# Prompt attention of a hybrid decoder layer: value products by twos, four slots for turned weights, and a new order of rows, turns and values

## The reference

```python
def block(i):                                   # 128 queries at a time
    s = (einsum('bqhd,bkhd->bhqk', qn, k_nope)  # 16 heads, 64 + 32 wide
         + einsum('bqhr,bkr->bhqk', qp, k_pe)) * ATTN_SCALE
    s = where(key_pos[None, :] <= q_pos[:, None], s, finfo.min)
    p = softmax(s, axis=-1)
    return einsum('bhqk,bkhd->bqhd', p, v)      # values 64 wide
```

## Time and profile before

| what | value |
|---|---|
| runs (median, lowest, highest) | 2851.91, 2851.1, 2855.4 us |
| profiled execution | 2861.62 us, span 2859.8 us |
| mean granted TensorE clock | 0.987 of 2.4 GHz |
| PE, PEld busy | 2781.5 us (97%), 2532.8 us (89%) |
| DVE, ACT, POOL busy | 1500.8 us (52%), 752.1 us (26%), 1056.5 us (37%) |
| prompt attention: L1373, L1388, L1398 in the chain that ended last | 3%, 2%, 3% of the span |

### The profile page before, as it was taken

The page is one execution under the profiler, slowest core; times in us unless marked ns, Lnnn a source line. Parts: engine busy times, 40 slices in busy tenths (PEclk is TensorE's granted clock), DMA queues, the critical chain, the costliest instruction groups (busy, mean ns, idle before and its releaser), DMA issues.

```text
span 2859.8 us, 45005 instructions
## 1 busy us (share of the span) xinstructions
PE 2781.5 (97%) x18648; PEld 2532.8 (89%) x18648; DVE 1500.8 (52%) x2075; ACT 752.1 (26%) x1182; POOL 1056.5 (37%) x611
## 2 busy tenths in 40 slices
PE   7999999999999999999999899999999999999998
PEld 7999999998999896666666599999999999999998
DVE  3665888674766564555444447876642222222226
ACT  2221211363545543555423322101210000000000
POOL 2553333333333333555311123446433333333331
PEclk9999999999999999999999999999999999999999
DMA  5274223564756657444343524354211111111111
GB/s 145 92 273 168 83 83 115 173 182 145 182 154 176 162 161 177 109 104 125 144 181 151 187 93 143 110 182 123 68 45 45 45 45 45 45 48 48 45 52 61
DMA packets 332053, 337.13 MB, mean 118 GB/s; under 512 B 43168, under 2 KB 284069, under 8 KB 329638
## 3 DMA queue, kind: packets, MB, share of 16 engines
q1 hardware_dynamic: 266984, 211.97, 26.6%
q10 hardware_dynamic: 61302, 84.71, 8.3%
q0 software_dynamic: 3584, 37.75, 3.4%
HBM read 245.35 MB, written 89.02 MB: 117 GB/s over the span
## 4 chain that ended last, share of the span: by engine, by line
PE 56%; DVE 5%; ACT 2%; issue 2%; DMA 2%; ACTq 0%; POOL 0%; DVEq 0%; SPq 0%
PE ps L1042 35%; PE ps L1373 3%; PE ps L1236 3%; PE ps L1398 3%; PE ps L1388 2%; PE ps L1530 2%; PE ps L1487 2%; PE ps L1506 1%; PE ps L1654 1%; DMA kpb<-in_cache_kpe,pgx 1%; ACT prb L2067 1%; DVE alo L2761 0%; DMA gt<-d_z 0%; DMA d_y<-s_y 0%; DVE ytok L2987 0%
## 5 line engine op out<-in xcount | busy, mean ns | idle before, releaser
L841 POOL TENSOR_TENSOR whi<-raw,cst 128x1024 fp32r<-128x1024 f32 x160 | 319.6, 1998 | 1084.5 <-PE ps L1042 888.8
L843 POOL TENSOR_TENSOR wlo<-raw,whi 128x1024 fp32r<-128x1024 f32 x160 | 432.8, 2705 | 12.5
L1042 PE MATMUL ps<-ahi,whi 128*128 128x352 f32 x1728 | 376.4, 326 | 1.9 <-DVE alo L2761 1.9
L1042 PE MATMUL ps<-alo,whi 128*128 128x352 f32 x1728 | 376.5, 326 | 0.0
L1042 PE MATMUL ps<-ahi,wlo 128*128 128x352 f32 x1728 | 371.6, 324 | 0.0
L1042 PEld LDWEIGHTS ps<-ahi,whi 128*128 128x128 f32 x1728 | 295.3, 190 | 2.5 <-DVE alo L2761 2.5
L1042 PEld LDWEIGHTS ps<-ahi,wlo 128*128 128x128 f32 x1728 | 297.1, 190 | 0.0
L1042 PEld LDWEIGHTS ps<-alo,whi 128*128 128x128 f32 x1728 | 296.1, 189 | 0.0
L1236 PE MATMUL ps<-xhi,whi 128*128 128x352 f32 x768 | 255.2, 332 | 2.8 <-ACT zo L1904 2.8
L1236 PE MATMUL ps<-xlo,whi 128*128 128x352 f32 x768 | 249.5, 325 | 0.0
L1236 PE MATMUL ps<-xhi,wlo 128*128 128x352 f32 x768 | 247.7, 323 | 0.0
(11 more groups left out here) (378 smaller groups left out, 5052.5 us busy)
## 6 DMA issues: line engine op xcount, KB each, us to landing
raw<-in_w_in SPq DMA_DIRECT2D x61, 512.0 KB, 5.5
s_a<-d_acum SPq DMA_DIRECT2D x32, 512.0 KB, 7.2
d_xbc<-so ACTq DMA_DIRECT2D x24, 528.0 KB, 2.7
gt<-d_g SPq DMA_DIRECT2D x24, 528.0 KB, 3.6
raw<-in_w_ffn_gate SPq DMA_DIRECT2D x22, 512.0 KB, 3.8
raw<-in_w_ffn_up SPq DMA_DIRECT2D x22, 512.0 KB, 3.8
raw<-in_w_ffn_down SPq DMA_DIRECT2D x22, 512.0 KB, 3.7
d_z<-zo ACTq DMA_DIRECT2D x16, 528.0 KB, 5.0
```

Of the source, the lines that this page charges most:

```text
L841: pool.tensor_tensor(whi[s][:, :], raw[:, u], ones[:, 0:1].broadcast_to([P, UNIT]), ALU.mult).then_inc(sem("unit_hi"), k["unit_hi"].adds(1))
L843: pool.tensor_tensor(wlo[s][:, :], raw[:, u], whi[s][:, :].bitcast(F32), ALU.subtract).then_inc(sem("unit_split"), k["unit_split"].adds(1))
L1042: last = pe.matmul(ps[0:m, 3 * b + c, 0:width], w(j), x[:, j, at:at + width], start=i == 0, stop=i == n - 1)
```

## The change

- `weigh_two` takes two key blocks' values together, a block and the one below it. Before it, PE waits for the copies: `turned_since` says how many turns have been issued since the second of the two; 0 waits for all copies, 1 for all but the last.
- `ptb` has four slots for each head in place of two. The two new ones lie where the split weights of other stages and `wrow` lie. `slot_of` picks one: `(4G + 3 - kb_) % 4`.
- The order of rows, turns and values is written anew on PE, and the order of maxima, reciprocals, exponentials and copies on DVE and ACT with it. After a turn there now often stand one or two rows, or another turn, where a weigh stood. `head_out` of half 1 stands before the exponential of row (1,1), and that of half 0 between those of (1,6) and (1,7).
- SP waits for the last values (`o_ready` at 16) before it loads `wrow`.

```diff
@@ -448,11 +448,15 @@
-    ptb = [[ar(f"ptb{slot}{h}", [P, 512]) for h in range(2)] for slot in range(2)]
+    idle_weights = Arena(base + RAW * UNIT * 4)
+    ptb = [[at(f"ptb{slot}{h}", [P, 512]) for h in range(2)] for slot, at in enumerate((ar, ar, idle_weights, idle_weights))]
...
+    def slot_of(G, kb_):
+        return (4 * G + 3 - kb_) % 4
@@ -759,6 +763,7 @@
         next_weights(4)
+        sp.wait_ge(sem("o_ready"), HEADS)
@@ -1395,34 +1400,64 @@
+        def weigh_two(pp, G, kb_, turned_since):
+
+            for h in range(2):
+                pe.wait_ge(sem(f"pt_read{h}"), k[f"pt_read{h}"].value(turned_since))
+            weigh(pp, G, kb_)
+            weigh(pp, G, kb_ - 1)
+
         def later_rows(pp, final=False):
-            for i in range(8):
-                scores(pp, 1, i)
-                if i % 2 == 0:
-                    turn_probs(0, 3 - i // 2)
-                    if i:
-                        weigh(pp, 0, 4 - i // 2)
-                    elif not final:
-                        weigh(1 - pp, 1, 0)
+            scores(pp, 1, 0)
+            if not final:
+                weigh_two(1 - pp, 1, 1, 0)
+            turn_probs(0, 3)
+            scores(pp, 1, 1)
+            turn_probs(0, 2)
+            scores(pp, 1, 2)
+            weigh_two(pp, 0, 3, 0)
+            scores(pp, 1, 3)
+            turn_probs(0, 1)
+            scores(pp, 1, 4)
+            turn_probs(0, 0)
+            scores(pp, 1, 5)
+            weigh_two(pp, 0, 1, 0)
+            scores(pp, 1, 6)
+            scores(pp, 1, 7)
 
         def earlier_rows(pp, more=True):
-            for i in range(8):
+            def row(i):
                 if more:
                     scores(1 - pp, 0, i)
-                turn_probs(1, 7 - i)
-                if not more and stop >= 6:
+                elif stop >= 6:
                     turn_key_weights(i)
-                if i:
-                    weigh(pp, 1, 8 - i)
-                else:
-                    weigh(pp, 0, 0)
+
+            turn_probs(1, 7)
+            row(0)
+            turn_probs(1, 6)
+            row(1)
+            row(2)
+            turn_probs(1, 5)
+            weigh_two(pp, 1, 7, 1)
+            turn_probs(1, 4)
+            row(3)
+            row(4)
+            turn_probs(1, 3)
+            weigh_two(pp, 1, 5, 1)
+            turn_probs(1, 2)
+            row(5)
+            row(6)
+            turn_probs(1, 1)
+            weigh_two(pp, 1, 3, 1)
+            turn_probs(1, 0)
+            row(7)
@@ -1453,9 +1488,7 @@
-        for h in range(2):
-            pe.wait_ge(sem(f"pt_read{h}"), k[f"pt_read{h}"].same())
-        weigh(1, 1, 0)
+        weigh_two(1, 1, 1, 0)
@@ -1992,22 +2025,45 @@
         def later_rows(pair, final=False):
...
+            probs(1, 0)
+            turned(0, 3)
+            if not final:
+                head_out(1, pair - 1)
+            probs(1, 1)
+            turned(0, 2)
+            probs(1, 2)
+            probs(1, 3)
+            turned(0, 1)
+            probs(1, 4)
+            turned(0, 0)
+            probs(1, 5)
+            probs(1, 6)
+            head_out(0, pair)
+            probs(1, 7)
...
@@ -2591,22 +2647,50 @@
         def later_rows():
...
+            row_max(1, 0)
+            row_inverse(0, 7)
+            turned(0, 3)
+            row_max(1, 1)
+            row_inverse(1, 0)
+            turned(0, 2)
+            row_max(1, 2)
+            row_inverse(1, 1)
+            row_max(1, 3)
+            row_inverse(1, 2)
+            turned(0, 1)
+            row_max(1, 4)
+            row_inverse(1, 3)
+            turned(0, 0)
...
```

More of the change, by code:

```diff
@@ L1397, in weigh @@
             for h in range(2):
-                last = pe.matmul(ps[64 * h:64 * h + 64, 6 + G, c0 * P:512], vb[pp][h][:, kb_, :], ptb[kb_ % 2][h][:, c0 * P:512],
+                last = pe.matmul(ps[64 * h:64 * h + 64, 6 + G, c0 * P:512], vb[pp][h][:, kb_, :], ptb[slot_of(G, kb_)][h][:, c0 * P:512],
                                  start=first, stop=kb_ == 0, skip_group_check=True)
@@ L1984, in turned @@
             act.wait_ge(sem("t_ready1"), k["t_ready1"].next())
-            act.activation(ptb[kb_ % 2][1][:, c0 * P:512], ps[:, 5, c0 * P:512], ACT.Copy).then_inc(sem("pt_read1"), k["pt_read1"].adds(1))
+            act.activation(ptb[slot_of(G, kb_)][1][:, c0 * P:512], ps[:, 5, c0 * P:512], ACT.Copy).then_inc(sem("pt_read1"), k["pt_read1"].adds(1))
         def head_out(G, pair):
@@ L1994, in later_rows, with earlier_rows, row @@
         def later_rows(pair, final=False):
[L1995 to L2004, removed]
+            probs(1, 0)
[13 more added lines that the diff above has]
+            probs(1, 7)
+        def earlier_rows(more=True):
+            def row(i):
                 if more:
@@ L2008, in earlier_rows @@
                     key_weights(i)
-                if i == 1:
-                    head_out(0, pair)
+            turned(1, 7)
+            row(0)
+            turned(1, 6)
+            row(1)
+            row(2)
+            turned(1, 5)
+            turned(1, 4)
+            row(3)
+            row(4)
+            turned(1, 3)
+            turned(1, 2)
+            row(5)
+            row(6)
+            turned(1, 1)
+            turned(1, 0)
+            row(7)
         def key_weights(i):
@@ L2029, in _ @@
                                           k["att_stored"]: 64} | pairs(k, {"s_read": 16, "o_read": 2})) as i:
-            earlier_rows(i * 2)
+            earlier_rows()
             later_rows(i * 2 + 1)
-            earlier_rows(i * 2 + 1)
+            earlier_rows()
             later_rows(i * 2 + 2)
-        earlier_rows(HEADS // 2 - 2)
+        earlier_rows()
         later_rows(HEADS // 2 - 1)
-        earlier_rows(HEADS // 2 - 1, False)
+        earlier_rows(False)
         head_out(1, HEADS // 2 - 1)
@@ L2593, in turned, with row @@
             dve.wait_ge(sem("t_ready0"), k["t_ready0"].next())
-            dve.tensor_copy(ptb[kb_ % 2][0][:, c0 * P:512], ps[:, 4, c0 * P:512]).then_inc(sem("pt_read0"), k["pt_read0"].adds(1))
+            dve.tensor_copy(ptb[slot_of(G, kb_)][0][:, c0 * P:512], ps[:, 4, c0 * P:512]).then_inc(sem("pt_read0"), k["pt_read0"].adds(1))
         def later_rows():
-            for i in range(8):
+            row_max(1, 0)
[12 more added lines that the diff above has]
+            turned(0, 0)
+            for i in range(5, 8):
                 row_max(1, i)
-                row_inverse(*((1, i - 1) if i else (0, 7)))
-                if i % 2 == 0:
-                    turned(0, 3 - i // 2)
+                row_inverse(1, i - 1)
         def earlier_rows(more=True):
-            for i in range(8):
+            def row(i):
                 if more:
@@ L2608, in earlier_rows @@
                     row_inverse(*((0, i - 1) if i else (1, 7)))
-                turned(1, 7 - i)
+            turned(1, 7)
+            row(0)
+            turned(1, 6)
+            row(1)
+            row(2)
+            turned(1, 5)
+            turned(1, 4)
+            row(3)
+            row(4)
+            turned(1, 3)
+            turned(1, 2)
+            row(5)
+            row(6)
+            turned(1, 1)
+            turned(1, 0)
+            row(7)
         for i in range(8):
```

## The result

| | before | after |
|---|---|---|
| median (lowest to highest), us | 2853.45 (2851.1 to 2855.4), 6 runs | 2871.78 (2867.8 to 2882.13), 6 runs |
| ratio | | 1.0063, 95% interval 1.0049 to 1.0077 |
| profiled execution, its span | 2861.62, 2859.8 | 2873.77, 2872.0 |
| first scores to the end of the stage | 1095.82 to 1397.76 = 301.9 | 1100.22 to 1409.16 = 308.9 |
| stage end to the second decode sequence's first transposes | 22.8 | 28.8 |

The changed kernel is 0.63% slower, some 18 us. The forecast was 2854 with a range up to 2863 and no change as the likeliest; both are wrong.

A forecast was written before the change was run, and what follows sets the result against it. PE was taken to bound the stage, ACT's order only just behind; +2.0 (seven repeats) - 0.6 - 0.5 - 0.6 (ends) + 2.0 (load) = +2.3 us on the profiled 2861.62, put on the median: 2854, range 2844 to 2863.

The forecast's parts named there:

- (d): First later half, last pair, and last round behind DVE's two additions: -0.6, -0.5 and -0.6 us.
- (e): wrow's load goes out ahead of ACT's last att store, delaying DVE's decode stage: +2 us, bounds 0 and +5.3.
- (c): New PE waits in each repeat: 3.9 us where 1.3 were, +2.6; with (a) and (b) a repeat of 35.8.
- (a): Six value pairs for twelve single ones on PE: -0.94 us a repeat, and -0.55 from fewer gaps.
- (b): Nine score groups start behind transposes, hiding their weight load: -0.85 us a repeat, bounds 0 and -0.85.
- rival 2: Weight load behind a transpose not hidden, (b) gives nothing: 2859, chance 0.20; sign: seven-block mask 1.34 after load, not 1.24.
- A: PE's wait ahead of the values of early blocks 3 and 2, for ACT's copy: 1.2 us a repeat.
- B: PE's wait in the turn of early block 0, second head, for a copy: 0.65 us a repeat.
- C: PE's wait at the next pair's first row, which needs the banks of row (1,6): 0.8 us a repeat.
- D: PE's wait in the turn of later block 6, second head, for block 7's copy behind `head_out`: 1.1 us a repeat.
- E: PE's wait at the turn of later block 4, first head, for DVE's copy of block 5: 0.2 us a repeat.
- rival 3: wrow's load takes the DMA engines whole, last store lands after 8.4 us: +5.3, 2857; chance 0.10, alone or with rival 2.

The follow-up runs named there:

- split kernel: Changed kernel with wrow's load behind prompt_over, three of six value pairs taken apart, the second block's values behind the next turn; ratio 1.0070.
- the changed kernel again: The changed kernel itself, unaltered, rerun as base of the second group; ratio 1.0062 to the kernel before.
- the mended load: Changed kernel with wrow loaded behind prompt_over, after the last att store; run twice, ratios 1.0031 and 1.0039, the second 2866.54 us.
- filled: Unread products in PE's waits A, C and D: on the changed kernel 1.0058; on that with the mended load 1.0029, 2866.71 us.
- the four profiles of the changed order: Profiles of the changed kernel (1.0063), the changed kernel again (1.0062), and the mended load twice (1.0031, 1.0039).
- the two of the old order: Profiles of the kernel before (median 2853.45 us) and of the late load alone (1.0021).
- the late load alone: The kernel before with one line of the change: SP waits for all values before loading wrow; ratio 1.0021, +6.0 us by the ratio.

## Why the prediction was wrong

Four steps of the sum failed. (d), the ends, had the last pair at -0.5 and the seventh repeat at -0.6 where they cost +1.7 and, falls included, +2.7. The granted clock wasn't in the sum: falls cost +1.6 in the five middle repeats. (e), the load, had +2 where it cost +6. And (c) had a repeat 0.3 us short. They are taken in turn, and some 4 to 7 us of the 18 stay open.

**(a), value pairs: right.** A pair of four blocks each takes 1.87 us from start to start. The gap behind a mask, which had no row, is 0.17 (1260.09 to 1260.26 in the changed kernel's timeline); I took 0.09 within bounds of 0 to 0.2. The split kernel prices the whole, with (b), at 0.35 and 0.44 a place for 0.41.

**(b), scores behind turns: right, against rival 2.** T[4] and S[7] together take 1.72; worked out were 0.5 + 1.24 = 1.74, and 1.84 if the load is not hidden. The sign I gave for it was badly put, and by its letter the 1.33 seen would be rival 2: the load goes out ahead of the last transpose, so the mask stands 1.33 behind the load (1264.21 to 1265.54) as it did behind values, and the gain is in the turn's own 0.39 (1263.82 to 1264.21), where it was 0.59. The rule of the Trainium skill that I weighed here (TensorE: Matmul & The Clock Gate, The mechanism, in Part 3) also names a background weight buffer as a way for a load to overlap; the trace agrees with that half of it, and not with the half that wants another row group: the scores' load has 96 rows and the transpose ahead of it 128. Which buffer a load goes to, no run shows.

**(c), the new waits: right in place and nearly in size, the repeat a little short.** A came out at 1.2 and a gap of 0.17 (1.34 in all), B at 0.5 for 0.65, C at 0.8 as walked, D at 1.0 for 1.1, E at 0.3 for 0.2: 3.8 for 3.9. The fall of the repeat when A and B, or D, were taken away was hit to 0.1 us twice. The forecast's 35.8 still was 36.1. Of the 0.3 between, 0.2 is the first head of block 0's turn, which waits for DVE's copy of block 1 (0.22 from row (1,4)'s mask to it, where other turns stand 0.02 behind a mask), and 0.2 is the gap behind a mask at 0.17 for 0.09 in three places. +0.6 on 35.55 is +4.2 over seven repeats where I had +2.0.

**(d), the ends: wrong, by a slip and a size.** In the last pair I counted the saving of its earlier half and left out that its later half carries A and B as every other: the later half went from 16.94 to 18.97, the earlier one from 18.19 to 17.85. The undisturbed last pair is 36.8 (the changed kernel again, and both with the mended load) against 35.1: +1.7 where I had -0.5. The seventh repeat, with DVE's additions, was to gain 0.6 by cover from C and D. It has no such cover: filled and without a fall it takes 37.99, 1.86 above its neighbours, where before it was 1.35 above. Over the four profiles of the changed order it is 39.6 on the mean, +2.7, falls included. The first pair gained more than I said, 39.7 on the mean of the four against 43.9 and 43.1 in the two of the old order, but with a different stretch at the low clock in each; what of it is the order isn't shown.

**The clock: not in the sum at all.** Each wait was priced by its length. PE had 1.3 us of waiting in a repeat and the clock never fell in the middle repeats; with 3.9 it fell in one or two of five, at 1.25 us each (37.4 against 36.15). The stages of the four profiles last 308.9, 306.3, 308.0 and 305.0 us: +5.1 on the mean over 301.9, where the terms of the sum had +0.3. By repeats: +3.0 by walk in the five middle ones, +1.6 by their falls (five in 20 repeats, 1.25 each), and -4.2, +2.7 and +2.1 for the first, the seventh and the last.

**(e), the load: right in kind, a third in size.** +2 was taken inside bounds of 0 and +5.3. The store landed 7.5 us after its issue and not 5, near rival 3, and DVE started 4.5 us later than before (7.7 for 3.2). The bounds themselves failed, because they end with DVE's start; the clock falls while PE stands idle, and the stretch as a whole grew by 6.0 (the change) to 6.8 (the late load alone). The ratios say +6.0 for adding it and -7 to -9 for taking it away. The Trainium skill (DMA: Bandwidth & Descriptors, Queues, rings and completion order) says that a DMA's completion lands only after every earlier write of that DMA engine, across its queues. By that rule the store waits for as much of the 2 MB as was ahead of it, and the 7.5 us agree; they would agree as well with two transfers that share the same engines, and no run here tells the two apart.

**The sum.** Stage +5.1 and load +6.0 make +11 of the 18. With the load mended the stage alone has to carry +9 and +11 by the ratios, and the traces give it 5. So 4 to 7 us have no place in the traces. Single profiles are no finer than that: the code ahead of the stage is the same in all kernels, and yet the stage began anywhere between 1095.8 and 1102.8 us. The clock over the whole execution bears on it. The mean granted clock of the runs is 0.990 before, 0.986 for the changed kernel again and 0.987 with the load mended, and among the runs of the kernel before 0.001 of it goes with 1.5 to 3 us. Part of that is counted above already: the stage of the four profiles has 22 us at 1.2 GHz on the mean, that of the two in the old order 14 and 17, which makes 0.0012 of the execution. The profiles go the same way: that of before ran at 0.987 and 8 us above its median, that of the second mended load at 0.990 and 7 us below. Whether idle time in one stage lowers the clock in a later one stays open: the filled kernel's runs stood at 0.989, near the clock of before, and were not measurably faster.

## What to carry over

- On an in-order engine that copies for another, put the copy ahead of the long instruction that nobody waits for yet. Here PE's work in a repeat shrank by 2.1 us and its waits grew by 2.7, nearly all of it behind ACT; the same pairs with the copies first and `head_out` later make the repeat 1.9 us shorter than before.
- When the order changes, walk each engine that a turn or a product waits for, and walk the first and last rounds whole: the slip in the last pair cost the forecast 2 us, and the cover counted on in the seventh repeat 1 more.
- Look at what a moved DMA goes out ahead of. A 2 MB load 0.6 us ahead of a small store that gates the next stage cost 6.0 to 6.8 us here; 3 us behind the store it cost the stretch nothing.

## What the runs showed of the hardware

- A small store issued 0.6 us behind a 2 MB load took 7.5 us to land in the changed kernel and 7.4 in the kernel before with that one edit (7.2 to 7.5 in the four others with the load there); with the load issued behind it, it took 2.0 to 3.2.
- Where PE stood idle for some 4 us, the granted clock was down for 6.8 to 10.2 us (1.2 GHz): the stretch lost 2 us more than the wait. Behind two waits of 0.8 and 1.0 us, with 2 us between their ends, the clock fell for 3.4 us, but in five of 20 middle repeats; with products of 384 and 512 columns in the waits it fell in none of ten.
- A weight load behind a transpose is hidden at 2.4 GHz as it is at 1.2: T[4] and S[7] together took 1.72 us, where 1.84 was worked out if it were not.
- Taking the falls away in one stage moved no median beyond its noise, twice (2872.08 for 2873.14, 2866.71 for 2866.54).
